# Three FFN boundaries of a two-block transformer kernel, made for the latents first and then for the context

## The reference, cut to what matters

```python
def swiglu(h, w_i, w_o):
    g, u = jnp.split(h @ w_i, 2, axis=-1)
    return (jax.nn.silu(g) * u) @ w_o

def trunk_layer(xl, xc, ...):            # latents, context
    xl = xl + 0.5 * g1l * swiglu(modulate(rmsnorm(xl, norm_w[0]), sh1l, sc1l), w_ffn1_in, w_ffn1_out)
    xc = xc + 0.5 * g1c * swiglu(modulate(rmsnorm(xc, norm_w[0]), sh1c, sc1c), w_ffn1_in, w_ffn1_out)
    hl = modulate(rmsnorm(xl, norm_w[1]), sh2l, sc2l)
    hc = modulate(rmsnorm(xc, norm_w[1]), sh2c, sc2c)
    mix_l, mix_c = token_mixer(hl, hc, w_in, ...)
    xl = xl + g2l * mix_l
    xl = xl + 0.5 * g3l * swiglu(modulate(rmsnorm(xl, norm_w[2]), sh3l, sc3l), w_ffn2_in, w_ffn2_out)
    if not last:                         # the context too, in the first layer
        ...
```

## Time and profile before

| what | value |
|---|---|
| median of 3 runs | 4288.41 us (4286.97 to 4290.26) |
| profiled execution, its own time | 4287.59 us |
| its span, first to last instruction | 4285.8 us |
| mean granted TensorE clock | 0.993 |
| TensorE matmul busy | 98% of the span |
| VectorE, ScalarE, GpSimd busy | 72%, 42%, 31% |

### The profile page before, as it was taken

How to read it: one execution, slowest core, us unless ns; L and a number is a source line. 1 busy time by engine, 2 the same in 40 slices (tenths; PEclk the granted TensorE clock), 3 DMA queues, 4 the chain that set the end, 5 groups by cost and what they waited for, 6 DMA issues and landing times.

```text
span 4285.8 us, 61414 instructions
## 1 busy us (share of the span) xinstructions
PE 4187.1 (98%) x24279; PEld 3729.0 (87%) x24279; DVE 3071.4 (72%) x4936; ACT 1793.0 (42%) x2976; POOL 1331.9 (31%) x699
## 2 busy tenths in 40 slices
PE   7999999999999999999999999999999999999999
PEld 5888778888888799867999999999999799998887
DVE  5775558877887686465599798788887675554776
ACT  3233352233233544263234786333334645444444
POOL 0000200000000100000378666777772058444443
PEclk9999999999999999999999999999999999999999
DMA  7543215544555364212477899999994166678884
GB/s 276 221 165 146 84 43 203 223 179 191 220 194 203 109 253 184 79 40 77 142 243 250 301 342 343 367 359 353 358 352 166 60 199 220 226 245 285 288 287 168
DMA packets 287199, 926.35 MB, mean 216 GB/s; under 512 B 19648, under 2 KB 171328, under 8 KB 212800
## 3 DMA queue, kind: packets, MB, share of 16 engines
q1 hardware_dynamic: 250048, 788.18, 51.8%
q0 software_dynamic: 36864, 134.23, 8.7%
HBM read 837.40 MB, written 84.93 MB: 215 GB/s over the span
## 4 chain that ended last, share of the span: by engine, by line
PE 86%; DVE 5%; DMA 4%; ACT 2%; POOL 1%; issue 1%; SPq 0%; ACTq 0%; POOLq 0%; DVEq 0%
PE bank L1132 25%; PE bank L1133 24%; PE bank L1134 24%; PE bank L1570 3%; DMA gates<-work 1%; PE bank L1325 1%; PE bank L1127 1%; PE bank L1122 1%; PE bank L1118 1%; PE bank L1337 1%; POOL weight_ring_low L2906 1%; PE bank L1362 1%; DVE work L2635 1%; DVE weight_ring_low L2246 1%; DMA work<-in_up_rows,work 1%
## 5 line engine op out<-in xcount | busy, mean ns | idle before, releaser
L2906 POOL TENSOR_TENSOR weight_ring_low<-weight_ring,up_high 128x1024 fp32r<-128x1024 f32 x233 | 586.4, 2521 | 1069.7 <-ACT up_high L1994 1067.6
L1134 PE MATMUL bank<-peer_h_high,weight_ring_low 128*128 128x256 f32 (+2 forms) x2240 | 698.3, 312 | 0.0
L1132 PE MATMUL bank<-peer_h_high,up_high 128*128 128x384 f32 (+1 forms) x2048 | 643.4, 314 | 14.3 <-POOL weight_ring_low L2906 7.4
L1133 PE MATMUL bank<-h_low,up_high 128*128 128x384 f32 (+1 forms) x2048 | 633.8, 309 | 0.0
L2081 ACT ACTIVATE down_high<-weight_ring 128x1024 fp32r<-128x1024 f32 x256 | 257.1, 1052 | 523.5 <-PE bank L1134 518.0
L1134 PE MATMUL bank<-h_high,weight_ring_low 128*128 128x512 f32 (+1 forms) x1280 | 463.9, 362 | 0.0
L1132 PE MATMUL bank<-h_high,in_high 128*128 128x512 f32 (+1 forms) x1216 | 441.1, 363 | 0.3
L1133 PE MATMUL bank<-h_low,in_high 128*128 128x512 f32 (+1 forms) x1216 | 440.8, 362 | 0.0
L2870 POOL TENSOR_SCALAR h<-work,params 128x256 f32<-128x256 f32 x12 | 11.8, 997 | 1376.7 <-PE bank L1477 874.6
L2662 DVE TENSOR_TENSOR weight_ring_low<-weight_ring,down_high 128x1024 fp32r<-128x1024 f32 x128 | 314.8, 2459 | 160.8 <-ACT down_high L2081 160.8
L1134 PEld LDWEIGHTS bank<-peer_h_high,weight_ring_low 128*128 128x128 f32 x2240 | 426.4, 190 | 3.7
(11 more groups left out here) (417 smaller groups left out, 10074.5 us busy)
## 6 DMA issues: line engine op xcount, KB each, us to landing
weight_ring<-in_up SPq DMA_DIRECT2D x128, 1024.0 KB, 6.0
weight_ring<-in_down SPq DMA_DIRECT2D x128, 1024.0 KB, 5.6
weight_ring<-in_mod_w SPq DMA_DIRECT2D x112, 1024.0 KB, 4.8
weight_ring<-in_ffn_in SPq DMA_DIRECT2D x88, 1024.0 KB, 6.9
weight_ring<-in_ffn_out SPq DMA_DIRECT2D x64, 704.0 KB, 5.7
gates<-work SPq DMA_DIRECT2D x40, 1024.0 KB
gelu<-work SPq DMA_DIRECT2D x64, 384.0 KB
work<-gates SPq DMA_DIRECT2D x32, 768.0 KB, 12.8
```

Of the source, the lines that this page charges most:

```text
L1132: mm(dst, w_high, a_high, start=first, stop=False)
L1133: mm(dst, w_high, a_low, start=False, stop=False)
L1134: return mm(dst, w_low, a_high, start=False, stop=last)
L2906: G.tensor_tensor(ring_low[:, slot, w], ring[:, slot, w], up_high[:, n % 3, :].bitcast(F32), ALU.subtract)\
```

## The change: what it does

At the three boundaries the last output panel is made in two passes over its 22 terms, for the latents into bank 3 and then for the context into bank 5 (`halved_panel`). Between the two passes TensorE waits until the square of chunk 6 is joined, because that square lies in bank 4 or 5. Behind the latents' pass VectorE adds them to x, ScalarE squares them, VectorE joins this last square too (`join_last`), and TensorE makes the column sums and the spread scales of the latents inside the context's pass, behind terms 4 and 9. There is one set of sums for each half, of squares that are all joined, in place of two for both.

Behind the panel the first four blocks are made for the latents (`halved_products`: high by high for all eight chunks, with the context's sums behind chunk 5, then high by low, with the context's spread behind chunk 2, then the low weights), and then for the context. Units 0 and 1 of the next stage's weights are rounded into the latent columns of work space whose context columns are still being read. The matmuls of `keep_busy` and TensorE's drains at these boundaries are gone.

```diff
@@ pe @@
+            def halved_products(name, s, blocks):
+                ...
+                for kc in range(KC):
+                    pe.wait_ge(half_rounded, m0 + kc + 1)
+                    for bank, k, j0, cols in blocks:
+                        mm(ps[bank][:, LAT], unit_block(k, j0 + kc), high[:, kc, LAT], start=kc == 0, stop=False)
+                    if kc == 5:
+                        pe.wait_ge(half_joined, 2 * ns["half"] + 2)
+                        column_sums(ns, norm, (2, 3)).then_inc(summed, 1)
+                for kc in range(KC):
+                    pe.wait_ge(half_split, m0 + kc + 1)
+                    ...
+            def halved_panel(before, early_bank, terms, part, splits, first_half):
+                norm, ns = before
+                last = len(terms) - 1
+                for n, term in enumerate(terms):
+                    if n in splits:
+                        pe.wait_ge(out_split, splits[n])
+                    o = split_product(ps[early_bank][:, LAT], *part(term, LAT), n == 0, n == last)
+                o.then_inc(half_done, 1)
+                pe.wait_ge(squares_added, at[norm]["joined"] + KC - 2)
+                for n, term in enumerate(terms):
+                    o = split_product(ps[ns["late_bank"]][:, CTX], *part(term, CTX), n == 0, n == last)
+                    if n == first_half:
+                        o.then_inc(out_half, 1)
+                    if n == 4:
+                        pe.wait_ge(half_joined, 2 * ns["half"] + 1)
+                        column_sums(ns, norm, (0, 1)).then_inc(half_summed, 1)
+                    if n == 9:
+                        pe.wait_ge(half_inverted, ns["half"] + 1)
+                        spread_scales(ns["scale_bank"], (0, 1)).then_inc(half_spread, 1)
+                o.then_inc(panel_done, 1)
...
-                barrier(pe, "pe", i, wait=False)
+                if stop is not None or "half" not in s and "half" not in norm_of.get(name, (name, {}))[1]:
+                    barrier(pe, "pe", i, wait=False)
@@ act @@
+            def halved_norm(name, s):
+                ...
+                act.wait_ge(half_added, n + 1)
+                act.wait_ge(squares_added, at[name]["joined"] + KC - 2)
+                A(total[:, LAT], x[:, kc, LAT], ACT.Square).then_inc(half_squared, 1)
+                round_unit(*s["next"], 0)
+                act.wait_ge(half_summed, n + 1)
+                root(slice(0, 2), half_rooted)
+                for kc in range(KC):
+                    act.wait_ge(half_scaled, n * KC + kc + 1)
+                    normalise(half_h[:, kc, :], high[:, kc, LAT], kc, 0, half_normed, half_rounded, n * KC + kc + 1)
+                    if kc == 3:
+                        act.wait_ge(x_added, at[name]["added"])
+                        A(total[:, CTX], x[:, s["order"][KC - 1], CTX], ACT.Square).then_inc(squares_ready, 1)
+                    if kc == 6:
+                        act.wait_ge(summed, at[name]["summed"] + 1)
+                        root(slice(2, 4), root_ready)
+                for kc in range(KC):
+                    act.wait_ge(scaled_ready, at[name]["scaled"] + kc + 1)
+                    normalise(h[:, kc, CTX], high[:, kc, CTX], kc, 1, normed, h_rounded, at[name]["normed"] + kc + 1)
+                round_unit(*s["next"], 2)
@@ dve @@
+            def halved_end(before, early_bank, gate, last_panel):
+                ...
+                dve.wait_ge(half_done, n + 1)
+                add(early_bank, LAT, 0).then_inc(half_added, 1)
+                join_last(norm, ns, LAT, 1)
+                round_second(*ns["next"])
+                dve.wait_ge(half_rooted, n + 1)
+                V.reciprocal(norm_scale[:, 0:2], square_sum[:, 0:2]).then_inc(half_inverted, 1)
+                dve.wait_ge(half_spread, n + 1)
+                ...
+                for k in range(KC):
+                    V.tensor_tensor(half_h[:, k, :], x[:, k, LAT], ps[ns["scale_bank"]][:, LAT], ALU.mult).then_inc(half_scaled, 1)
+                dve.wait_ge(panel_done, last_panel)
+                add(ns["late_bank"], CTX, 1).then_inc(x_added, 1)
+            def halved_norm(name, s):
+                ...
+                for kc in range(6):
+                    half_low(kc)
+                    if kc == 3:
+                        join_last(name, s, CTX, 2)
+                dve.wait_ge(root_ready, at[name]["root"] + 1)
+                V.reciprocal(norm_scale[:, 2:4], square_sum[:, 2:4]).then_inc(inverse_ready, 1)
+                for kc in range(6, KC):
+                    half_low(kc)
+                split_unit(*s["next"], 0)
+                split_unit(*s["next"], 1)
+                dve.wait_ge(panel_done, plan.panel0[name] + 1)
+                for kc in range(KC):
+                    V.tensor_tensor(h[:, kc, CTX], x[:, kc, CTX], ps[s["late_scale"]][:, CTX], ALU.mult).then_inc(scaled_ready, 1)
+                    if kc >= 3:
+                        low(kc - 3)
+                ...
+                split_unit(*s["next"], 2)
...
                     join_squares(name, dc - 1)
+                    if dc == KC - 1 and "half" in norm_of[name][1]:
+                        halved_end(norm_of[name], dc % 4, s["gate"], p0 + 2 * FC + KC)
+                        continue
                     dve.wait_ge(panel_done, p0 + 2 * FC + dc + 1)
```

More of the change, by code:

```diff
@@ L478, in build @@
         h_rounded, h_split = sem("h_rounded"), sem("h_split")
+        half_done, half_added, half_squared, half_summed = (sem(f"half_{n}") for n in ("done", "added", "squared", "summed"))
+        half_joined = sem("half_joined")
+        half_rooted, half_inverted, half_spread, half_scaled = (sem(f"half_{n}") for n in ("rooted", "inverted", "spread", "scaled"))
+        half_normed, half_rounded, half_split = (sem(f"half_{n}") for n in ("normed", "rounded", "split"))
         up_rounded, up_split, up_split_dve = sem("up_rounded"), sem("up_split"), sem("up_split_dve")
@@ L544, in build @@
                 s["sums"] = 2 if s["joined"] else 3 if s["pooled"] else KC
-                if kind == "norm":
+                if kind == "norm" and i + 1 < len(stages):
                     s["next"] = stages[i + 1][1:]
+                if before == "ffn" and s.get("t") == T and "next" in s:
+                    s["sums"] = 1
+                    s["half"] = sum("half" in other for _, _, other in stages[:i])
+                    s["late_bank"], s["late_scale"] = 5, 4
+                    stages[i + 1][2]["halved"] = name, s
                 norm_of[stages[i - 1][1]] = name, s
@@ L803, in squares_of @@
                 return work[:, k % (2 * T // t) * t:k % (2 * T // t) * t + t]
+            if k == KC - 1 and "half" in s:
+                return ps[s["late_scale"]][:, :]
             if k in (0, KC - 1):
@@ new lines, in column_sums, with spread_scales @@
+            def column_sums(ns, norm, tiles):
+                for tt in tiles:
+                    i = mm(ps[ns["sum_bank"]][:, tt:tt + 1], squares_of(norm, ns, 0)[:, tt * P:tt * P + P], ones[:, 0:1],
+                           start=tt % 2 == 0, stop=True, skip_group_check=True)
+                return i
+            def spread_scales(bank, tiles):
+                for tt in tiles:
+                    i = mm(ps[bank][:, tt * P:tt * P + P], norm_scale[:, tt:tt + 1].to_broadcast([P, P]), ident, start=True, stop=True)
+                return i
@@ L1209, in joined_sums @@
             def joined_sums(name):
-                if name not in norm_of:
+                if name not in norm_of or "half" in norm_of[name][1]:
                     return
@@ L1243, in norm_stage @@
             def norm_stage(name, s):
-                if s["before"] == "mods":
+                if s["before"] == "mods" or "half" in s:
                     return
@@ L2253, in split_chunk, with join_last @@
                     .then_inc(h_split, 1)
+            def join_last(norm, ns, cols, n):
+                if n == 1:
+                    dve.wait_ge(half_squared, ns["half"] + 1)
+                else:
+                    dve.wait_ge(squares_ready, at[norm]["square"] + KC)
+                dve.wait_ge(squares_added, at[norm]["joined"] + KC - 2)
+                total = squares_of(norm, ns, 0)[:, cols]
+                V.tensor_tensor(total, total, squares_of(norm, ns, KC - 1)[:, cols], ALU.add).then_inc(half_joined, 1)
@@ L2255, in norm_stage @@
             def norm_stage(name, s):
+                if "half" in s:
+                    halved_norm(name, s)
+                    return
                 t, tiles = s.get("t", TL), s.get("t", TL) // P
```

97 lines of the change are left out of this document (92 added, 5 removed).

## The result

| | before | after |
|---|---|---|
| median of 20 runs each, side by side, us | 4293.8 | 4304.1 |
| lowest and highest, us | 4286.83, 4300.98 | 4296.06, 4308.75 |
| profiled execution: span, us | 4285.8 | 4297.5 |
| mean granted clock of TensorE | 0.993 | 0.991 |

The ratio of the times is 1.0025, with a 95% interval of 1.0018 to 1.0031. The change costs 10.7 us (7.7 to 13.3) on 4293.8. It is slower, by 0.25%; whether by more than 0.2% the interval leaves open.

The account below looks back on a forecast made before the run. TensorE, busy for 98% of the span, was taken as the bound. A gain of 1.1 us and losses of 5.8 and 4.6 at the three boundaries sum to a 9.3 us loss: 4298 against the median 4288.41, range 4291 to 4304.

Parts of the forecast that it names:

- (1): Split of columns at the boundaries: 0.0132 us more a pair of 256-column matmuls, 438 pairs, 5.8 us of added TensorE time.
- (2): Sums and fillers at each boundary: four new column-sum tiles and four new spread tiles, 1.8 us a boundary.
- (3): Removal of TensorE's drains between last product and sums: priced at nothing, bounds 0 and 0.5 us a boundary.
- (4): Wait between panel 7's two passes: TensorE idles 1.2, 6.4 and 5.3 us until square 6 is joined.
- (5): From the gate G, before the context's pass, to the opening blocks' end: 35.0 us, 32.0 at the third boundary.
- (6): Behind the second and third boundary's idles: 4.2 us of half-rate clock, 1.8 us each, bounds 1.3 and 2.3.
- the second rival: Latents' short waits and the unit 2 wait also lower the clock, 1.8 us a fall: 4302 to 4305; chance 0.16.

Follow-up runs that it names:

- six panels: The changed kernel with the modulation products dealt out over panels 0 to 5 in place of 0 to 6; 4284.57 us against 4292.61 of before, 0.9983.
- the two single runs: The changed kernel, once with unit 2 rounded early (4308.97 us), once with TensorE's drains at the three boundaries put back (4302.71 us).
- fillers: The changed kernel with 13 and 11 filler matmuls between panel 7's two passes at the second and third boundary; 4298.86 us, 1.0011 of before.
- the control: The kernel before with the modulation products dealt out over panels 0 to 5; 4297.75 us, 1.0009 of before.

## Why the prediction was right, and where it was not

The direction, the mechanism and the size of the loss were right: slower by about 0.2%, with VectorE's join behind the modulation products as the gate. The absolute time was not: 4304.1 lies above the range of 4291 to 4304, and the terms that failed are the base and the clock behind the wait for unit 2. By its own steps:

**(1), the columns.** A product of 256 columns starts every (4.00 - 0.28) / 31 = 0.120 us at 412.25, and 0.120 in the split passes, as forecast. With a fixed part of 2.5 ns, as in the section "Wait — 56ns, not 53.3ns?" of the Trainium skill's page "TensorE: Matmul & The Clock Gate", it would be an estimated 0.115, half of the 0.2268 + 0.0025 of a wide one; the trace does not agree with that.

**(2), sums and spread.** Inside the context's pass the latents' sums hold TensorE for 0.45 us (394.98 to 395.55, less one pitch) and their spread for 0.44 (397.22 to 397.78, less one pitch). Twice that, for both halves, is the 1.8 us forecast.

**(3), drains at nothing.** Nothing shows in the one run with them put back.

**(4), the gate.** Counted from the start of panel 7 it opens at 9.07, 14.21 and 13.12 us; the forecast's times give 9.2, 14.3 and 13.2. TensorE stood for 1.01, 6.13 and 5.05 us against 1.2, 6.4 and 5.3. The run with six panels shows that this is the cause: open the gate and the loss of 8.9 us at the second and third boundary becomes a gain of 5.5.

**(5), from the gate to the end.** The first latent chunk is rounded at 399.4, G + 6.3, against G + 6.1; ScalarE makes one every 0.95 us; TensorE waits for them 0.20 and 0.69 us. From the gate to the end the first boundary took 34.53 us where I had 35.0. Without the 0.4 for two late followers my sum was 34.6, so that term was one too many; at full clock the first product behind the gate starts its follower 0.11 us late (393.08 to 393.31, against 0.120) and not 0.2. Unit 2 was late by 1.80 us where I had 2.

**(6), the clock.** It fell behind both long waits, and to a pitch of 0.213 us as forecast. I took 4.2 us of it, 1.8 us each, and the kernel after had 1.27 and 1.52; the two single runs had 2.2 to 2.5. So 1.8 was in the middle of what occurs, and both of my bounds, 1.3 and 2.3, were crossed.

| us | forecast | after |
|---|---|---|
| first boundary | -1.1 | -1.63 |
| second | +5.8 | +4.79 |
| third | +4.6 | +4.15 |
| boundaries | +9.3 | +7.3 |
| clock behind the wait for unit 2 | not in the sum | about +1.4 |

The last line was the second rival, of which one part came true. A mean of 0.60 over 4 us is 3.2 us of half rate, and that is 1.4 us at least, since it may go on behind the window. The other part of that rival did not: the short waits in the latents' high products left the clock at 1.00, as the earlier trace rows had said. So the rule in the section "A second HAM failure mode: psum-queue depth-cycling" of the Trainium skill's page "TensorE: Matmul & The Clock Gate" found no case here in the group of short waits, while the one wait of 1.80 us in front of unit 2 had a fall behind it in three of four traces (after, six panels, fillers; not with the drains put back). Together with it the change costs 8.7 us in the trace, within the measured 7.7 to 13.3. That this lies so near to the 9.3 of the forecast is in part luck: the boundaries lost 2.0 us less than I had summed, and the fall that I had left out gave 1.4 back. The rest of the 11.7 us between the spans is not shown to be the change's: 0.98 before the first boundary, where the start of panel 7 lies between 382.47 and 384.62 in the nine traces and latest in the control, which is without the change; and 1.74 in mix_0, which is told below.

**What failed** is a step that I treated as bookkeeping: that the profiled execution's time "lies 0.8 us under the median of 4288.41, against which the forecast is 4297.7". That median was of three runs. The twenty runs beside the kernel after have a median of 4293.8 and reach from 4286.83 to 4300.98. The other two sets of runs of before, 35 and 16, have medians of 4292.61 and 4293.19. The base was thus 5.4 us too low, and the range of 4291 to 4304 was made of the doubts about the change alone, with nothing in it for the base. A loss of 9.3 us on 4293.8 is 4303.1, 1 us from the 4304.1 measured. The second term that failed is the clock behind the wait for unit 2: the sum had TensorE stand there for 2 us and put the fall behind it at nothing, leaving it to a rival of 0.16; it was about 1.4 us.

## What to carry to other kernels

To start a norm early by making half of a panel first moves its start to the moment at which the helping engine comes to it. So read that engine's program from the start of the panel to the join, and count what stands ahead: here eight products of 1.22 us, harmless as long as the join had 15 us until TensorE asked for it, made a gain of 5.5 us into a loss of 8.9 at two boundaries. One constant that moved them a panel earlier, and one weight unit rounded a loop earlier, turned 10.7 us slower into 13.3 us faster. And before a difference of 0.2% is forecast as an absolute time, the base wants more than three runs.

## What the runs showed of the hardware that I had not expected

The length of the half-rate stretch is not set by the idle time in front of it alone. Behind the same wait of 6.13 us the second boundary lost 1.27 us in the kernel after and 2.4 and 2.5 in the two single runs, in which VectorE and TensorE do the same up to that gate but for the drains.

An idle time of 1.75 us lets the clock fall in one execution and not in another. In mix_0 TensorE stands for 1.75 us (up to 564.58 in the kernel before) and for 1.79 us 16 us later; both are of the same length in the kernels before, after and with the first boundary alone. Windows of these two places in the kernel before:

```profile
565.00:570.00 5.00, 5.00 (x33) 3.97 (x33) 2.86 (x6) 3.24 (x6) 0.00 (x0) 0.66 0.00 0
580.00:585.00 5.00, 3.90 (x17) 3.25 (x18) 3.56 (x5) 1.88 (x3) 0.00 (x0) 1.00 0.58 210
```

of the kernel after:

```profile
565.00:570.00 5.00, 5.00 (x27) 4.09 (x28) 2.26 (x6) 3.07 (x5) 0.00 (x0) 0.67 0.00 0
580.00:585.00 5.00, 4.48 (x14) 3.57 (x15) 2.98 (x5) 1.30 (x2) 0.00 (x0) 0.70 0.52 205
```

and of the kernel with the first boundary alone:

```profile
564.00:569.00 5.00, 5.00 (x32) 4.09 (x28) 1.78 (x4) 3.11 (x5) 0.00 (x0) 1.00 0.00 0
...
579.00:584.00 5.00, 5.00 (x16) 3.97 (x16) 1.02 (x2) 0.00 (x0) 0.00 (x0) 0.66 0.19 80
```

The clock fell in the first place, in both, and in the second alone. Each fall is worth about 1.5 us: the stretch between the first two boundaries took 538.3 to 538.5 us in four of the nine traces and 539.8 to 540.0 in five. The kernel with fillers has one of the short ones with the same code up to there as the kernel after, so I take it for luck of the execution. That it comes as often with the change as without is not shown (all five long ones have the change, as have two of the four short ones), and neither is what decides it.

The stretch behind the third boundary took from 2907.3 to 2921.0 us in the nine traces, in code that the runs did not change. That is as wide as the spread of the twenty runs of before (14.2 us). Most of it is idle time of TensorE: it is without a product in flight for 76.7 to 77.2 us of this stretch in the three longest (2917.6 to 2921.0, the control among them) and for 67.3 to 72.6 us in the six others. In the control its longest wait there is one of 8.4 us for VectorE's split of a weight unit (line 2662), where the longest of before is 4.0. Why that split comes late in some executions stays open.
